# Tails behind the experts of a two-layer decoder trunk: sums transposed unscaled, root and weight applied later, row loads by half, the last scaling on three engines

## The reference

```python
def rms_norm(x, w):
    xf = xf * lax.rsqrt(jnp.mean(xf * xf, axis=-1, keepdims=True) + RMS_EPS)
    return (xf * w.astype(jnp.float32)).astype(x.dtype)

for layer in range(DEPTH):
    h = rms_norm(x, norm_mix_w[layer])
    mix = even_mixer(h, ...) if layer % 2 == 0 else retention_mixer(h, ...)
    x = x + mix
    h = rms_norm(x, norm_ffn_w[layer])
    x = x + hierarchical_moe(h, ...)      # 16 experts, two for each token
return rms_norm(x, final_norm_w)

def retention_mixer(h, w_in, norm_w, w_out):
    q, k, v, g = split_cols(h @ w_in, ODD_SPLITS)
    q, k = rotary(q), rotary(k)           # products with cos and sin of the position
    o = multiscale_retention(q, k, v)
    o = rms_norm(o, norm_w) * jax.nn.silu(g)
    return merge_heads(o) @ w_out
```

## Time and profile before

| | |
|---|---|
| runs, median (lowest to highest) | 1202.81 us (1201.90 to 1204.03), 3 runs |
| the profiled execution: span | 1207.7 us |
| PE busy | 1119.9 us, 93% |
| DVE, ACT, POOL busy | 687.4, 596.7, 416.2 us |
| share of the chain of waits | PE 86%, DVE 6%, ACT 3%, DMA 2%, POOL 1% |
| mean granted TensorE clock | 0.962 |

### The profile page before, as it was taken

How to read it: one execution, slowest core, us unless ns; L and a number is a source line. 1 busy time by engine, 2 the same in 40 slices (tenths; PEclk the granted TensorE clock), 3 DMA queues, 4 the chain that set the end, 5 groups by cost and what they waited for, 6 DMA issues and landing times.

```text
span 1207.7 us, 19553 instructions
## 1 busy us (share of the span) xinstructions
PE 1119.9 (93%) x7019; PEld 919.5 (76%) x7019; DVE 687.4 (57%) x977; ACT 596.7 (49%) x873; POOL 416.2 (34%) x348
## 2 busy tenths in 40 slices
PE   6998999999999699998899999999999996999980
PEld 4786887778788588886778888888888885788870
DVE  3434434358743899995617442453432136999975
ACT  4555234251433489996332433233342233899971
POOL 4343311210123144445253335442334331344442
PEclk8998999999999799999899999999999997999995
DMA  9232311112216599995642222322222363999955
GB/s 253 59 86 55 70 38 37 53 36 72 71 26 228 182 342 378 375 366 210 235 131 88 79 79 78 115 88 73 85 70 88 100 193 115 359 374 377 366 205 217
DMA packets 89283, 194.73 MB, mean 161 GB/s; under 512 B 20157, under 2 KB 21241, under 8 KB 88186
## 3 DMA queue, kind: packets, MB, share of 16 engines
q1 hardware_dynamic: 67562, 159.87, 39.6%
q10 hardware_dynamic: 11856, 17.07, 4.1%
q0 software_dynamic: 9792, 16.80, 3.7%
HBM read 189.50 MB, written 23.07 MB: 176 GB/s over the span
## 4 chain that ended last, share of the span: by engine, by line
PE 86%; DVE 6%; ACT 3%; DMA 2%; issue 2%; POOL 1%; POOLq 0%; SPq 0%; DVEq 0%; ACTq 0%
PE ps L663 25%; PE ps L665 24%; PE ps L664 24%; PE ps L2412 2%; PE ps L2204 2%; PE ps L2057 1%; DMA arena<-y 1%; PE ps L2089 1%; PE ps L2340 1%; DMA arena<-hs,slot_rows 1%; DVE arena L1433 1%; DMA x<-in_x_dram 1%; PE ps L2033 1%; PE ps L2020 1%; PE ps L2482 1%
## 5 line engine op out<-in xcount | busy, mean ns | idle before, releaser
L827 POOL TENSOR_TENSOR wl<-raw,wh 128x1024 fp32r<-128x1024 f32 x98 | 238.5, 2441 | 408.4 <-ACT wh L991 408.1
L663 PE MATMUL ps<-wh,hT_hi 128*128 128x512 f32 x864 | 348.2, 403 | 3.9 <-DVE hT_lo L1886 2.4
L665 PE MATMUL ps<-wh,hT_lo 128*128 128x512 f32 x864 | 339.4, 393 | 0.0
L664 PE MATMUL ps<-wl,hT_hi 128*128 128x512 f32 x864 | 338.9, 392 | 0.0
L991 ACT ACTIVATE wh<-raw 128x1024 fp32r<-128x1024 f32 x116 | 122.7, 1068 | 220.2 <-PE ps L665 201.5
L663 PEld LDWEIGHTS ps<-wh,hT_hi 128*128 128x128 f32 x864 | 163.6, 189 | 39.4 <-issue 4.6
L665 PEld LDWEIGHTS ps<-wh,hT_lo 128*128 128x128 f32 x864 | 163.2, 189 | 34.6
L664 PEld LDWEIGHTS ps<-wl,hT_hi 128*128 128x128 f32 x864 | 163.7, 189 | 30.8
L663 PE MATMUL ps<-hT_hi,wh 128*128 128x512 f32 x288 | 117.6, 408 | 8.8 <-ACT arena L1154 6.0
L1861 DVE TENSOR_TENSOR wl<-arena,wh 128x1024 fp32r<-128x1024 f32 x96 | 114.3, 1223 | 5.0 <-ACT wh L1250 2.8
L1861 DVE TENSOR_TENSOR wl<-raw,wh 128x1024 fp32r<-128x1024 f32 x92 | 109.5, 1224 | 11.4 <-ACT wh L991 4.8
(11 more groups left out here) (323 smaller groups left out, 1575.3 us busy)
## 6 DMA issues: line engine op xcount, KB each, us to landing
raw<-in_moe_w_gate_up_dram SPq DMA_DIRECT2D x64, 512.0 KB, 10.7
arena<-in_moe_w_gate_up_dram SPq DMA_DIRECT2D x64, 512.0 KB, 10.3
raw<-in_odd_w_in_dram SPq DMA_DIRECT2D x48, 512.0 KB, 3.7
raw<-in_even_w_in_dram SPq DMA_DIRECT2D x32, 512.0 KB, 4.7
arena<-in_moe_w_down_dram SPq DMA_DIRECT2D x32, 512.0 KB, 11.7
raw<-in_moe_w_down_dram SPq DMA_DIRECT2D x32, 512.0 KB, 14.0
arena<-y ACTq DMA_DIRECT2D x8, 1024.0 KB, 8.4
raw<-in_odd_w_out_dram SPq DMA_DIRECT2D x16, 512.0 KB, 3.5
```

What stands on the lines that cost most here:

```text
L663: nc.tensor.matmul(dst, lh, rh, start=first, stop=False)
L664: nc.tensor.matmul(dst, lh, rl, start=False, stop=False)
L665: return nc.tensor.matmul(dst, ll, rh, start=False, stop=last)
L827: pool.tensor_tensor(columns_of(i, wl[:, i % NSPL, :, :]), raw_columns(i), columns_of(i, wh[:, i % NSPL, :, :]).bitcast(F32), ALU.subtract ...
```

## The change

In both tails:

- POOL reads the overflow flag and signals `y_all_stored` right behind the last scatter; ACT itself waits for the scatters to land. All four remainders of block 10 are issued on POOL behind that.
- The load of tile 0 is two DMAs of 512 KB with a semaphore each.

In norm 2:

- PE transposes `X` itself (`x_ready`: the tile's second sum). The norm's weight is applied at the evacuation, where a feature is a partition: for each block of 128 columns one ACT instruction and one DVE instruction with a scalar for each partition (`nw1`), four of each to a group.
- The token's root is applied behind the products: in the evacuations of the values (`rv`) and gates (`rg`), and by a new step `roots` for query and key: ACT makes four diagonal matrices of the roots, PE spreads them over the partitions by four fp32 matmuls, DVE multiplies `cos_t` and `sin_t` by the result. It stands between the rows of block 10 and their evacuation.
- PE's order: a row is run in two halves, the second half behind the next tile's transposes. 18 and 4 filler calls in place of 26 and 3.

In norm 4:

- POOL multiplies tiles 0 and 1 by the weight, ACT scales them by the root; DVE scales tile 2, and tile 3 in two halves. Outputs go out as they are ready, five DMAs.

```diff
@@ schedule @@
-            s += [("rows", b, t) for t in range(NT)] + [("evac", b)]
+            s += [("rows", b, t) for t in range(NT)] + [("roots",), ("evac", b)]
@@ POOL, end of moe @@
                 for par in range(2):
                     scatter(NE // 2 - 1, par, 32 * l + 31 + par)
-                    free_last(NE // 2 - 1, par)
-                for i in range(2):
-                    lo(m + 6 * NE + i)
-                free_last(NE // 2, 0)
-                for q in range(2):
-                    pool.wait_ge(s_(f"xg_loaded{q}"), 144 * (l + 1))
-
-                pool.nop().then_inc(s_(f"ov_stored{l}"), 1)
+                    if par == 0:
+                        free_last(NE // 2 - 1, par)
                 n = overflow_flag(pool, l)
                 with pool.If(n > 0):
+                    for q in range(2):
+                        pool.wait_ge(s_(f"y_stored{q}"), 128 * (l + 1))
+                        pool.wait_ge(s_(f"xg_loaded{q}"), 144 * (l + 1))
+                    pool.nop().then_inc(s_(f"ov_stored{l}"), 1)
...
                 pool.nop().then_inc(s_("y_all_stored"), 1)
-                for i in range(2, 4):
+                for i in range(4):
                     lo(m + 6 * NE + i)
+                free_last(NE // 2 - 1, 1)
+                free_last(NE // 2, 0)
+                for q in range(2):
+                    pool.wait_ge(s_(f"xg_loaded{q}"), 144 * (l + 1))
@@ POOL, norm 4 @@
+                elif step[0] == "norm" and step[1] == 4:
+                    pool.wait_ge(s_("wb_loaded"), 64)
+                    for T in range(2):
+                        pool.wait_ge(*x_ready(4, T))
+                        L(pool.tensor_tensor(fin(T), X[:, T, :], wb(4), ALU.mult), s_("fin_scaled"))
+                        norm_scale(4, T)
+                    norm_scale(4, 2)
+                    norm_scale(4, 3)
@@ ACT @@
+                    if n == 2:
+                        for j in range(4):
+                            k = 4 * g + j
+                            A(act.activation(HTH[:, k, cols(T)], tile(name)[:, cols(j)], ACT.Copy, scale=nw1[:, k:k + 1]),
+                              s_("hT_hi_made") if j == 3 else None)
+                        continue
...
+                if n == 4:
                     for T in range(NT):
                         square(n, T)
+                        if 0 < T < 3:
+                            last(T - 1)
...
+            def last(T):
+                act.wait_ge(s_("fin_scaled"), T + 1)
+                act.wait_ge(s_("norm_r"), 16 + T + 1)
+                A(act.activation(fin(T), fin(T), ACT.Copy, scale=rs[:, T:T + 1]), s_("fin_act"))
+
+            def roots():
+                act.wait_ge(s_("norm_r"), 8 + NT)
+                for T in range(NT):
+                    A(act.activation(rdiag[:, cols(T)], ident[:, :], ACT.Copy, scale=rs[:, T:T + 1]), s_("rs_diag"))
...
-                            A(act.activation(rv_half(t, 0), src, ACT.Copy), s_("rv_hi"))
+                            A(act.activation(rv_half(t, 0), src, ACT.Copy, scale=rs[:, t:t + 1]), s_("rv_hi"))
...
-                            A(act.activation(gt[:, t % 2, :], src, ACT.Silu), rd)
+                            A(act.activation(gt[:, t % 2, :], src, ACT.Silu, scale=rs[:, t:t + 1]), rd)
...
                 act.wait_ge(s_("y_all_stored"), l + 1)
+                for q in range(2):
+                    act.wait_ge(s_(f"y_stored{q}"), 128 * (l + 1))
                 src = y2_dram[l].rearrange("(T p j) d -> T p j d", p=P, j=2)
-                for T in range(NT):
+                act.dma_start(YP[:, 0, 0, :], src[0][:, 0, :]).then_inc(s_("yp_loaded0"), 16)
+                act.dma_start(YP[:, 0, 1, :], src[0][:, 1, :]).then_inc(s_("yp_second0"), 16)
+                for T in range(1, NT):
                     act.dma_start(YP[:, T, :, :], src[T]).then_inc(s_(f"yp_loaded{T}"), 16)
@@ DVE @@
+                if n == 2:
+                    combine(0, 0, 0)
+                    combine(0, 0, 1)
+                    combine(0, 1, 0)
+                    dve.wait_ge(s_("wb_loaded"), 32)
+                    for T in range(NT):
+                        lo_tiles(("hT", n, T), T)
+                        if T == 0:
+                            combine(0, 1, 1)
+                        if T + 2 < NT:
+                            combine(0, T + 2, 0)
+                            combine(0, T + 2, 1)
+                    return
+                if n == 4:
+                    for T in range(NT):
+                        for j in range(2):
+                            combine(1, T, j)
+                    dve.wait_ge(s_("wb_loaded"), 64)
+                    dve.wait_ge(s_("norm_r"), 16 + 3)
+                    D(stt(fin(2), X[:, 2, :], rs[:, 2:3], wb(4), ALU.mult, ALU.mult), s_("fin_dve"))
+                    dve.wait_ge(s_("norm_r"), 16 + 4)
+                    for hf in range(2):
+                        c = slice(512 * hf, 512 * hf + 512)
+                        D(stt(fin(3)[:, c], X[:, 3, c], rs[:, 3:4], wb(4)[:, c], ALU.mult, ALU.mult), s_("fin_dve"))
+                    return
...
+            def roots():
+                tile_is_ready(dve, "roots")
+                dve.wait_ge(s_("ret_consts"), 48)
+                D(tt(cos_t, cos_t, tile("roots"), ALU.mult))
+                D.read(tt(sin_t, sin_t, tile("roots"), ALU.mult), "roots")
...
+                    if name[0:2] == ("hT", 2):
+                        for j in range(4):
+                            k = 4 * g + j
+                            ins = stt(lo[:, j, :], tile(nm)[:, cols(j)], nw1[:, k:k + 1], hi[:, j, :].bitcast(F32), ALU.mult, ALU.subtract)
@@ PE @@
-                    keep_busy(26)
+                    keep_busy(18)
...
+                    if n == 2:
+                        if T == 0:
+                            keep_busy(4)
+                        if T > 0:
+                            rows(MOE_AT[0], T - 1, (2, 3))
+                        rows(MOE_AT[0], T, (0, 1) if T < NT - 1 else (0, 1, 2, 3))
+
+            def roots():
+                pe.wait_ge(s_("rs_diag"), NT)
+                t = open_tile("roots")
+                for T in range(NT):
+                    ins = mm(t[:, cols(T)], onec.broadcast_to([P, P]), rdiag[:, cols(T)], start=True, stop=True)
+                done(ins)
```

103 lines of the change are left out of this document (56 added, 47 removed).

## The result

The changed kernel took **1211.59 us** (median of 4 runs, 1211.08 to 1214.2), the kernel before 1202.76 beside it (4 runs): a ratio of 1.0072, 95% interval 1.0058 to 1.0086. It is 8.8 us slower, where 1204.0 was forecast and 1208.2 was the top of the range. The profiled execution has a span of 1210.0 us. The two profiled spans can't be subtracted: 1210.0 - 1207.7 is only 2.3.

What follows compares the result with a forecast made beforehand. TensorE was taken as the bound, 93% busy, leaving only the waits behind both layers' experts. Middle +1.9 us (-1.4 + 3.3) and end -0.7 gave +1.2, so 1204.0 us; range 1198.0 to 1208.2, likeliest case 1202 to 1206.

Steps and rivals of the forecast that it cites:

- (d): Middle, sums to first row: small instructions cost 1.3 us a group on ACT, 1.5 on DVE; first row 583.7, before 590.06.
- (e): Middle, rows in halves: PE idles 1.4 us three times, 28.9 us for 23.9; rows end 612.6, 1.4 us sooner.
- (f): Handover, rows to next block: uncovered roots step takes 4.6 us for 1.29, cost 3.3; scalings moved into evacuations cost nothing.
- the rivals: Two alternatives: slower by the clock, 1207.0 us, chance 0.28; faster because the POOL-DVE shut-out doesn't bind, 1198.8, chance 0.20.
- the end: Kernel's end, last scatter to finish: earlier load and lighter DVE, mostly given back to POOL's products; gain 0.7 us.
- (a): Middle: the row load is issued sooner, at the scatter's landing, 570.15 for 571.34; gain 1.2 us.
- (b): Middle: tile 0 loaded in two halves, the first landing after 3.9 us at 574.05, the second at 575.4.
- (c): Middle: POOL's weight products shut out DVE's sums; the second sum ends at 578.7, before 579.26, unhindered 576.7.
- the rival's clock: Behind the handover: new PE waits halve the clock, so 6 us of dense matmuls do 3 us of work; chance 0.28.
- the slower rival: Handover waits of 1.2 and 2.5 us cost PE its full clock: +4.2 us in all, 1207.0; chance 0.28.
- the clock rival: Same as the slower rival: half clock behind the handover, 1207.0 us, chance 0.28.
- The rival "slower": Same as the slower rival: waits around the roots' matmuls cost the clock, 1207.0 us, chance 0.28.

Runs made afterwards that it cites:

- experiment 5: The changed kernel with POOL's third and fourth remainder products in layer 0's tail waiting for tile 0's two sums: 1211.49 us, ratio 1.0079.
- experiment 4: The changed kernel with norm 2's weight left out, so one ACT and one DVE instruction of 128x512 a group: 1205.07 us, ratio 0.9999.
- experiment 7: The changed kernel with the roots step beside block 11's first piece and the weight as one DVE product per group: 1202.17 us, ratio 0.9977.
- experiment 10: The changed kernel with 3 filler matmuls ahead of the roots' matmuls and 4 behind, into a free bank: 1210.98 us, ratio 1.0052.
- experiment 2: The changed kernel with the last norm as before (four DVE scalings, one output DMA a tile, no POOL weight products): 1211.57 us, ratio 1.0056.
- experiment 1: The changed kernel with the roots step moved behind block 10's evacuation, beside block 11's first piece: 1208.3 us, ratio 1.0028.
- experiment 6: The kernel before, only with the last norm's four roots taken from POOL to ACT and DVE: 1202.55 us, ratio 0.9986.
- experiment 8: The kernel of experiment 7 with POOL's products held as in experiment 5, last norm as before, its roots on ACT and DVE: 1200.71 us, ratio 0.9978.
- experiment 9: The kernel of experiment 8 without the hold on POOL's products: 1197.44 us, ratio 0.9940.
- experiment 3: The kernel before with only the early flag, ACT's own wait for the landing and tile 0's load in halves, both tails: 1204.74 us, ratio 1.0008.

## Why the prediction was wrong

The sum missed by 6.3 us in the trace (+7.5 for +1.2), in four places: the rows 2.7, because ACT's small instructions were priced too low in (d) and (e); the handover's own work 0.8, in (f); the clock 2.0, which the sum had at nothing and the rivals named; and the end 0.6. The other 0.2 stands behind the handover.

**(a), (b), (c): the mechanism right, the time in part by luck.** The load is issued 0.1 us behind the landing (565.33 to 565.43), though the scatter landed 0.4 us later than before, so 0.7 and not 1.2 us is gained. The first half took 3.97 us (3.9 forecast, though "in proportion to bytes" doesn't give it: half of 5.29 is 2.6, and 3.9 was a choice between 3.5 and 5.3). The first sum lasted 2.74 us beside POOL's product, and the second ended at +14.13; the forecast 578.7 is +14.16. That these meet is luck: the half landed at +10.05 and not +9.51, and from the first sum's start to the second's end it took 4.05 us and not 4.65. The order was another as well. The forecast let the first sum finish in 1.28 us and then held the second behind POOL's fourth product (by 9.27 us for four the third ends at 573.95, so 574.05 lies in the fourth, not in the third as (c) says); measured, the first sum was held until that product's end at 571.07 and ended 1.1 us behind it, and the second ran free in 1.30. Experiment 5, with both sums at 1.28 us each once POOL's product is out of the way, shows the shut-out as the cause of 1.3 us. The Trainium skill (GPSIMD Engine Reference, section 1, Specifications) names contention over interfaces to SBUF that POOL shares with DVE instructions of two SBUF inputs; the rows of the chain agree, with 2.74 us for 1.28.

**(d): the term of the small ACT instructions was too small.** ACT's 128x128 with a scale took 0.368 us and the next began 0.40 behind the start of the one before; I had 0.28 and 0.04, 0.32 together, from a line through 0.60 and 0.38, drawn on to a quarter of the size, over instructions without a scale. By the rows it was the scale and not the size: at 512 columns the copy of block 10's values takes 0.595 us without a scale (L1200 before) and 0.688 with one for each partition (L1246 after), 0.09 more, and 0.28 + 0.09 is the 0.37 that was measured. For DVE the form had been priced, and 0.351 and 0.385 were as forecast (0.34, 0.38). The first row came at +19.83, not +19.16. The Trainium skill (VectorE: DVE Perf Modes, section on the TRN2 errata) warns of small tiles for instructions that read SBUF; these read PSUM, and the splitting cost here too. The estimate from its table for ScalarE from PSUM (0.25 us for 128 columns) is farther off than my line: 0.368 was measured. Nor would it have made the stage 0.5 us shorter, as (d) has it: 0.03 us less an instruction, in the four that DVE waits for, is 0.1.

**(e): the rows, forecast to end 1.4 us sooner, ended 1.3 later (+50.77).** The mechanism is the one described, three idles between half rows, 1.74 us each and not 1.4. The cycle took 8.4 us where 7.8 was forecast: 0.7 from the transposes to ACT's first rounding (0.45), 1.67 for ACT's group (1.4), 3.17 for DVE (3.1). Three cycles (1.8) and the late first row (0.7) make 2.5 of the 2.7 us. Experiments 4 and 7 show the cause: with whole groups the three waits vanish, and the rows end 7.0 and 6.2 us sooner.

**(f): the chain was right and short by a quarter, and the rival's clock came on top.** It was forecast at 4.6 us and took 6.0; 5.4 at full clock (experiment 10). The copies took 0.40 us each, not 0.31, and the roots' matmuls 1.16 us at full clock, not 0.9. Then the granted clock fell to 0.50 from 612.3 to 619.1. This was the slower rival, given 0.28. Its condition came true; its price, 3 us, was too high: 0.6 inside the handover and 1.4 behind (experiment 10), 2.0 together. My argument against it, that neither wait is as long as 2.71, does not hold. Nor does it take both waits: the clock fell 0.4 us behind the start of the roots' matmuls, behind the wait of 1.81 alone, and they took 1.77 us for 1.16. In experiment 2 it fell 0.6 us into them. But in experiment 5 the same matmuls behind the same wait of 1.81 ran at full clock, and only block 11, behind 2.43 us, at half; so it was in experiment 4 (1.52, then 2.44). Waits of 1.94 and 1.77 (experiment 1) left the clock at full. So block 11 began at half clock in all four traces with the wait of 2.4 us; behind 1.8 it went either way, and what decides there stays open.

**A term put at nothing.** Of the scalings by the root in the evacuations (f) says that they have the old shapes and cost nothing. They had another form: ACT's copy took 0.688 us for 0.595, DVE's remainder 0.751 for 0.69. Little of it shows in the time: with the clock kept full (experiment 10) the layer behind block 11's start was 0.3 us longer than before.

**The end: forecast at -0.7, measured -0.1.** The last sum gained 0.8 (1.2 forecast), held up as foreseen by two products on POOL (2.34 and 3.10 us). That gain is the load alone: tile 1 landed 0.8 us sooner behind the scatter. From tile 1's first sum to the last one DVE took 11.02 us, 11.06 before (1188.57 to 1199.63), although the scalings between were gone: two sums beside POOL's products took 2.46 and 3.25 us and gave 3.2 us back, as (c)'s mechanism says. What the sum had not priced at all is the program's closing. In all nine traces in which POOL makes the last roots, with either way of storing the output, the span ended 5.89 us behind POOL's last root; in the three without (experiments 6, 8, 9) it ended 0.45 us behind the last landing. So a last output in halves, landing sooner, wins nothing while POOL's root stands where it did.

**The sum.** Middle: rows +1.3 for -1.4, handover +4.7 for +3.3, behind it +1.6 for 0, of which 1.4 is the clock; end -0.1 for -0.7. That is +7.5 by the trace against +1.2. The four wrong terms all erred to the same side. The range's top, 1208.2, was the clock rival's 1207.0 with a little spread, so it held each miss alone and not both together: without the clock's 2.0 the trace has +5.5, near that top. The rival "slower" and the mis-sized small instructions are not exclusive: each had been priced as if the other terms held.

What stays open: 1.3 us between the traces' +7.5 and the medians' +8.8, which is inside the interval and mostly gone against the later runs of the kernel before; what decides on the clock behind a wait of 1.8 us; and why one of the second half loads in experiment 3 landed late.

## What to carry to other kernels

An instruction that is split must be priced at its own size, on its own engine and in its own form: here the line over sizes was good, and the scale for each partition, 0.09 us on ACT, was what it left out. Where no row has that form, the upper bound belongs into the sum, because in a cycle that the split sets every tenth of a microsecond comes back with each instruction and each round. A serial step through three engines between two dense stretches costs its whole length, plus, here, a stretch at half clock; put the same step beside work that doesn't need it. And compare two profiles from an instruction that both have, never by their spans.

## What was not expected of the hardware

- The end of the program stood 5.9 us behind POOL's last root in both kernels (1201.84 to 1207.7, 1204.14 to 1210.0). The last output had landed 1.8 and 2.2 us ahead of that end. With POOL idle since the last scatter (experiments 6, 8 and 9) it stood 3.1 us behind DVE's last instruction and 0.45 behind the last landing, and in experiment 6 the end came 2.1 us sooner relative to that scatter, though the last scaling was only 0.7 sooner.
- Two executions of the same code differed by 5 us before the first changed instruction, at granted clocks of 0.93 and 0.98 over the first 100 us.
- The same roots' matmuls behind the same wait of 1.81 us ran at half clock in one trace (1.77 us) and at full in another (1.16).
- Moving POOL's products away from DVE's sums only moved the meeting: 2.23 us for a 1.28 us sum, one instruction later.
